# The delta-rule mixer in four streams, laid under the convolutions, with the inverse's second orientation transposed from the first

## The reference

```python
def gated_deltanet_mixer(h, w_in, conv_w, a_log, dt_bias, norm_w, w_out):
    B, T, _ = h.shape
    H, Dh = GDN_HEADS, GDN_HEAD_DIM                      # 8 heads of 128
    proj = h @ w_in                                      # qkv 3072, z 1024, b 8, a 8
    ...
    qkv = jax.nn.silu(causal_dwconv(qkv, conv_w))        # width 4
    ...
    q = l2norm(q) * (Dh ** -0.5)
    k = l2norm(k)
    beta = jax.nn.sigmoid(b.astype(jnp.float32))
    g = -jnp.exp(a_log.astype(jnp.float32)) * jax.nn.softplus(
        a.astype(jnp.float32) + dt_bias.astype(jnp.float32))
    o = chunk_gated_delta_rule(q, k, v, g, beta)
    o = rmsnorm_2(o, norm_w) * jax.nn.silu(z.reshape(B, T, H, Dh))
    return o.reshape(B, T, GDN_V_DIM) @ w_out
```

## Time and profile before

| | us |
|---|---|
| median of 3 runs | 3209.63 (3208.53 to 3215.67) |
| the profiled execution | 3211.74 |
| its span | 3210.0 |
| PE busy | 2693.5 (84%) |
| DVE busy | 883.0 (28%) |
| ACT busy | 405.9 (13%) |

### The profile page before, as it was taken

One profiled execution on the slowest core, in us unless ns is written; L12 is line 12 of the kernel. 1 busy time (PEld: TensorE's weight loads), 2 busy tenths in 40 slices (PEclk: granted clock), 3 DMA queues, 4 the chain that ended last, 5 costly groups with the idle time before them and its releaser, 6 DMA issues.

```text
span 3210.0 us, 34641 instructions
## 1 busy us (share of the span) xinstructions
PE 2693.5 (84%) x13970; PEld 1520.1 (47%) x13970; DVE 883.0 (28%) x1880; ACT 405.9 (13%) x767; POOL 203.5 (6%) x267
## 2 busy tenths in 40 slices
PE   6987877789989987899799888888794779887886
PEld 3443445444444444544385434434664755444443
DVE  3144627510120045200224110110545544111111
ACT  1121212110010013100101000000122111000001
POOL 3111101110010020100011000000000001000000
PEclk9998997899999999999899998999897989989999
DMA  6655649254444441334543799999530025899997
GB/s 225 211 197 195 228 173 323 70 178 143 139 146 154 157 147 53 138 120 154 215 162 140 307 419 421 419 420 418 165 106 1 5 96 199 365 416 421 421 421 309
DMA packets 264854, 721.85 MB, mean 225 GB/s; under 512 B 15248, under 2 KB 149040, under 8 KB 210864
## 3 DMA queue, kind: packets, MB, share of 16 engines
q1 hardware_dynamic: 251232, 690.00, 56.4%
q0 software_dynamic: 13520, 30.41, 2.8%
HBM read 719.17 MB, written 1.18 MB: 224 GB/s over the span
## 4 chain that ended last, share of the span: by engine, by line
PE 65%; DMA 20%; DVE 9%; SPq 2%; issue 2%; ACT 2%; DVEq 0%; ACTq 0%
PE ps L872 22%; DMA ring<-in_moe_w_up 16%; PE ps L1496 9%; PE ps L982 7%; PE ps L897 5%; PE ps L1083 3%; PE ps L1065 3%; DMA ring<-in_ada_w 3%; SPq L532 2%; PE ps L1037 2%; DMA ring<-in_ffn_w_in 1%; PE ps L908 1%; PE ps L877 1%; PE ps L1486 1%; PE ps L1268 1%
## 5 line engine op out<-in xcount | busy, mean ns | idle before, releaser
L872 PE MATMUL ps<-ring,hT 128*128 128x512 f32 x1600 | 717.6, 603 | 49.7 <-DMA ring<-in_ffn_w_in 30.2
L872 PEld LDWEIGHTS ps<-ring,hT 128*128 128x128 f32 x1600 | 305.6, 194 | 417.2 <-issue 404.6
L1496 PE MATMUL ps<-arena 128*32 128x512 f32 x1536 | 275.8, 699 | 82.0 <-DMA ring<-in_moe_w_up 76.0
L1496 PE MATMUL ps<-ring,arena 128*32 128x512 f32 x512 | 275.1, 700 | 0.0
L1486 PEld LDWEIGHTS ps<-arena,h 128*128 128x128 f32 x1024 | 248.4, 334 | 15.3 <-issue 11.7
L1486 PE MATMUL ps<-arena,h 128*128 128x128 f32 x1024 | 244.9, 398 | 3.5 <-issue 3.5
L982 PE MATMUL ps<-ring,arena 128*128 128x512 f32 x528 | 232.2, 593 | 2.4 <-ACT arena L1725 2.4
L2162 DVE SCALAR_TENSOR_TENSOR arena<-ps,arena 128x256 f32<-128x256 f32 x66 | 28.1, 425 | 614.1 <-ACT arena L1721 613.9
L1496 PEld LDWEIGHTS ps<-arena 128*32 128x32 f32 x1536 | 67.6, 125 | 263.8 <-issue 180.7
L897 PE MATMUL ps<-hT,ring 128*128 128x256 f32 x768 | 171.3, 387 | 1.5 <-ACT hT L1659 1.5
L1037 PE MATMUL ps<-ring,cond 128*2 128x128 f32 (+1 forms) x3072 | 110.6, 307 | 66.7 <-DMA ring<-in_ada_w 61.7
(11 more groups left out here) (484 smaller groups left out, 2648.1 us busy)
## 6 DMA issues: line engine op xcount, KB each, us to landing
ring<-in_moe_w_down SPq DMA_DIRECT2D x128, 1024.0 KB, 17.7
ring<-in_ada_w SPq DMA_DIRECT2D x48, 2048.0 KB, 13.2
arena<-in_moe_w_gate SPq DMA_DIRECT2D x96, 1024.0 KB, 11.7
arena<-in_moe_w_up SPq DMA_DIRECT2D x96, 1024.0 KB, 9.8
ring<-in_ffn_w_in SPq DMA_DIRECT2D x66, 1024.0 KB, 8.6
ring<-in_ffn_w_out SPq DMA_DIRECT2D x33, 1024.0 KB, 5.0
ring<-in_moe_w_gate SPq DMA_DIRECT2D x32, 1024.0 KB, 15.7
ring<-in_moe_w_up SPq DMA_DIRECT2D x32, 1024.0 KB, 17.8
```

The source lines that it names most:

```text
L872: m = pe.matmul(o3, lhsT_of(k), ring[:, a:a + 2, k * EH:(k + 1) * EH], start=start and k == 0, stop=stop and k == KC - 1)
L1496: m = pe.matmul(ps[a * CAP:(a + 1) * CAP, 6, :].rearrange("p (u c) -> p u c", u=2), x_slots[:, k, a * CAP:(a + 1) * CAP], slot_pair(gate_s ...
```

## The change

The same mixer is written in another order and in parts with other operations.

- Under the 24 projection blocks now also run: b and a, the decays, their sums and running sums, the turning of finished q, k, v groups to tokens (`tokens_turned`), the squares for the norms (now on ACT, L2120 of the new program) with their sums, and the differences of the decays (`gap`). DVE makes block c's convolution before it gates block c - 1, the sigmoid has two buffers, and the note copies are gone.
- The four z blocks stand between the turnings and the scores instead of in one piece.
- All four pairs of head group and tile are streams (s = 0 to 3) of one run of levels. The first level has no products: D and DT are the identity less LM and less its transpose, which PE turns (`unit_turned`).
- From level 2 on only `D - D T` is a matmul. Its transpose, which the step needs as weights, is made by PE transposing D itself (`inverse_turned`) and an ACT copy. At the last level only the transposed result is made.
- The copies after the levels go to ACT. For tile 1 `q S` is scaled afterwards, not q before.
- The multiplication of z by the norm weights moves under the levels. Tile 0 of the output is projected before tile 1 is turned, and `arena_passed_on` is signalled after tile 1 is turned.
- The scratch of the streams also takes v_scale, v_shift and two tiles of x_sb.

```diff
-            for c in range(12):
...
+            def tokens_turned(g):
+                pe.wait_ge(sem("gd_conv"), 4 * g + 4)
+                for t in range(2):
+                    transposes([gT[:, 4 * g + q, t * P:(t + 1) * P] for q in range(4)])
+
+            def features_turned(t):
+                pe.wait_ge(sem("gd_norm"), t + 1)
+                for where, off in ((gtok, 8), (gkb, 0), (gtok, 0)):
+                    for hd in (0, 4):
+                        transposes([where[:, t, off + hd + a, :] for a in range(4)])
+
+            for j in range(12):
                 feature_major(SEQ, NT)
-            token_major(LAT)
-            token_major(LAT)
-            pe.wait_ge(sem("gdn_constants"), 16 * 6)
+                if j >= 2 and j % 2 == 0:
+                    tokens_turned(j // 2 - 1)
...
+            def unit_turned(s):
+                pe.wait_ge(sem("gd_lm"), LM_TURNED[s])
+                for a in range(4):
+                    m = pe.transpose(ps[:, 2 * s, a * P:(a + 1) * P], LM[s][:, a, :], ident[:, :])
+                m.then_inc(sem("gd_t"), 1)
+
+            def t_of(lvl, s):
+                pe.wait_ge(sem("gd_lm"), d_ready(lvl, s))
+                each(2 * s, lambda a: LM[s][:, a, :], lambda a: DD[s][:, a, :]).then_inc(sem("gd_t"), 1)
+
+            def inverse_turned(s):
+                for a in range(4):
+                    m = pe.transpose(ps[:, 2 * s + 1, a * P:(a + 1) * P], DD[s][:, a, :], ident[:, :])
+                m.then_inc(sem("gd_t"), 1)
+
+            def step_of(lvl, s):
+                pe.wait_ge(sem("gd_t_read"), turned_read(lvl, s))
+                if lvl + 1 < LEVELS:
+                    m = each(2 * s, lambda a: DT_[s][:, a, :], lambda a: TT[s][:, a, :])
+                else:
+                    m = each(2 * s + 1, lambda a: TT[s][:, a, :], lambda a: DT_[s][:, a, :])
+                m.then_inc(sem("gd_step"), 1)
+
+            z_block(0, 0)
+            tokens_turned(5)
+            z_block(0, 1)
+            features_turned(0)
+            z_block(1, 0)
+            pe.wait_ge(tp_evacuated, n.tp)
+            pe.wait_ge(sem("gd_gap"), 4)
+            scores(0)
+            scores(1)
+            features_turned(1)
+            unit_turned(0)
+            unit_turned(1)
+            z_block(1, 1)
+            pe.wait_ge(tp_evacuated, n.tp)
+            pe.wait_ge(gu_evacuated, n.gu)
+            scores(2)
+            scores(3)
+            t_of(1, 0)
+            t_of(1, 1)
+            unit_turned(2)
+            step_of(1, 0)
+            step_of(1, 1)
+            unit_turned(3)
+            t_of(1, 2)
+            t_of(1, 3)
+            step_of(1, 2)
+            step_of(1, 3)
+            for lvl in range(2, LEVELS):
+                for s in range(4):
+                    t_of(lvl, s)
+                for s in range(4):
+                    inverse_turned(s)
+                for s in range(4):
+                    step_of(lvl, s)
+
...
+                if t == 1:
+                    mixed_tiles(g_o, (1,))
+                    pe.wait_ge(tp_evacuated, n.tp)
+                    pe.matmul(ps[:, 4, 0:1], ident[:, :], ident[:, 0:1], start=True, stop=True).then_inc(sem("arena_passed_on"), 1)
+                for half in range(2):
+                    m = mixer_half(out_slots, t, half, t * P)
...
-                for lvl in range(LEVELS):
-                    for t in range(2):
-                        s0 = 2 * (LEVELS * g + lvl) + t
-                        pe.wait_ge(sem("gd_lm"), s0 + 1)
-                        for a in range(4):
-                            m = pe.matmul(ps[:, 3 * t, a * P:(a + 1) * P], LM[t][:, a, :], DD[t][:, a, :], start=True, stop=True)
-                        m.then_inc(sem("gd_t"), 1)
-                    for t in range(2):
-                        s0 = 2 * (LEVELS * g + lvl) + t
-                        pe.wait_ge(sem("gd_t_read"), s0 + 1)
-                        for a in range(4):
-                            pe.matmul(ps[:, 3 * t + 1, a * P:(a + 1) * P], DT_[t][:, a, :], TT[t][:, a, :], start=True, stop=True)
-                        for a in range(4):
-                            m = pe.matmul(ps[:, 3 * t + 2, a * P:(a + 1) * P], TT[t][:, a, :], DT_[t][:, a, :], start=True, stop=True)
-                        m.then_inc(sem("gd_step"), 1)
...
+            for lvl in range(1, LEVELS):
+                for s in range(4):
+                    act.wait_ge(sem("gd_t"), t_done(lvl, s))
+                    tell(nc.scalar.copy(TT[s], quarter(ps[:, 2 * s, :])), sem("gd_t_read"))
+                for s in range(4 if lvl >= 2 else 0):
+                    act.wait_ge(sem("gd_t"), t_done(lvl, s) + 4)
+                    tell(nc.scalar.copy(DT_[s], quarter(ps[:, 2 * s + 1, :])), sem("gd_t_read"))
...
-                tell(V.tensor_copy(note[:, :], eps_t[0:1, :]), sem("gd_pre"))
...
+            for c in range(24):
+                conv(c)
+                if c >= 1:
+                    conv_gated(c - 1)
+                if c == 4:
+                    ba_read()
+                if c == 6:
+                    decays_made()
+                if c == 11:
+                    sums_read()
+                if c in (13, 14):
+                    squares_summed(c - 13)
+                if 17 <= c < 21:
+                    gap(c - 17)
+                if c in (21, 22):
+                    squares_summed(c - 19)
+            conv_gated(23)
...
+            def scores_read(s):
+                dve.wait_ge(sem("gd_scores"), s + 1)
+                do(V.tensor_tensor(LT[s], b4(2 * s), LM[s], ALU.mult))
+                do(V.tensor_tensor(AT[s], b4(2 * s + 1), AT[s], ALU.mult))
+                tell(V.tensor_tensor(LM[s], LT[s], all4(lv[:, 0, :]), ALU.mult), sem("gd_lm"))
+
+            def first_level(s, turned):
+                tell(V.tensor_tensor(DT_[s], all4(ident[:, :]), LM[s], ALU.subtract), sem("gd_lm"))
+                dve.wait_ge(sem("gd_t"), turned)
+                tell(V.tensor_tensor(DD[s], all4(ident[:, :]), b4(2 * s), ALU.subtract), sem("gd_lm"))
+                tell(V.tensor_tensor(LM[s], LT[s], all4(lv[:, 1, :]), ALU.mult), sem("gd_lm"))
...
+            for lvl in range(1, LEVELS):
+                for pair in ((0, 1), (2, 3)):
+                    for s in pair:
+                        if lvl + 1 < LEVELS:
+                            dve.wait_ge(sem("gd_t"), t_done(lvl, s))
+                            tell(V.tensor_tensor(LM[s], LT[s], all4(lv[:, lvl + 1, :]), ALU.mult), sem("gd_lm"))
+                    for s in pair:
+                        dve.wait_ge(sem("gd_step"), step_done(lvl, s))
+                        if lvl + 1 < LEVELS:
+                            tell(V.tensor_tensor(DD[s], DD[s], b4(2 * s), ALU.subtract), sem("gd_lm"))
+                        else:
+                            tell(V.tensor_tensor(DT_[s], DT_[s], b4(2 * s + 1), ALU.subtract), sem("gd_inverse"))
+                if lvl in (2, 3):
+                    zt = g_z[:, lvl - 2, :].rearrange("p (a b) -> p a b", a=8)
+                    do(V.tensor_tensor(zt, zt, g_norm.rearrange("p (o b) -> p o b", o=1).broadcast_to([P, 8, P]), ALU.mult))
+
             for g in range(2):
```

More of the change, by code:

```diff
@@ new lines, in _, with z_block, each @@
+            z_units = [n.slots(2), n.slots(2)]
+            def z_block(half, t):
+                if t == 0:
+                    for s in z_units[half]:
+                        filled(s)
+                products(gu_bank(), lambda k: hT[:, k, SEQ + t * P:SEQ + (t + 1) * P], z_units[half]).then_inc(block_done, 1)
+            def each(bank, lhsT, rhs):
+                for a in range(4):
+                    m = pe.matmul(ps[:, bank, a * P:(a + 1) * P], lhsT(a), rhs(a), start=True, stop=True)
+                return m
@@ L1642, in _ @@
+            n.x += 2
             moe(1)
@@ new lines, in taken @@
+            def taken(dst, bank, count, done):
+                act.wait_ge(*count)
+                tell(nc.scalar.copy(dst, quarter(ps[:, bank, :])), done)
+            taken(TT[0], 0, (sem("gd_u"), 1), sem("gd_u_read"))
+            taken(TT[1], 2, (sem("gd_u"), 2), sem("gd_u_read"))
+            for g in range(2):
+                taken(TT[2 + g], 4 + 2 * g, (sem("gd_u"), 2 * g + 3), sem("gd_u_read"))
+                taken(LM[g], 1 + 2 * g, (sem("gd_u"), 2 * g + 4), sem("gd_u_read"))
+            for g in range(2):
+                taken(LM[2 + g], 5 + 2 * g, (sem("gd_o"), 2 * g + 1), sem("gd_batch"))
+                taken(g_o0[:, 4 * g:4 * g + 4, :], 2 * g, (sem("gd_o"), 2 * g + 2), sem("gd_batch"))
@@ L2873, in _ @@
[L2873 to L2876 removed]
+            z_gated(1, 1)
+            first_level(0, 1)
+            first_level(1, 2)
+            scores_read(2)
+            scores_read(3)
+            first_level(2, 5)
+            first_level(3, 6)
```

413 lines of the change are left out of this document (203 added, 210 removed).

## The result

| us | before | after |
|---|---|---|
| median | 3210.38 (4 runs, 3208.53 to 3215.67) | 3085.82 (4 runs, 3077.52 to 3091.33) |
| profiled execution | 3211.74 | 3081.46 |
| its span | 3210.0 | 3079.7 |

The ratio is 0.9607 with an interval of 0.9579 to 0.9635: 125 us less. I had forecast 3087.

A forecast was written before the change was run, and what follows sets the result against it. It took TensorE to bound the conv stretch and levels, VectorE parts between. Mixer 98.5 + 58.2 + 44.9 + 21.2 + 34.9 = 257.7 against 382.3, 124.3 less after rounding: 3087 us, range 3079 to 3094.

The forecast's parts named there:

- Step 1: Convolution stretch: 86.1 us of projections plus 12.4 of inserted TensorE work, 98.5 us; at most 3 more for table loads.
- Step 2: From the last conv projection to the first four-stream level: 58.2 us, TensorE's z blocks covering other work, then VectorE bounding.
- T: The end of the last conv projection block, 2363.97 us before the change and forecast at 2376.
- Step 3: Five levels of four streams, bound by TensorE: 9.3 us for the first, 8.9 for four more, 44.9 instead of 95.
- Step 4: Levels' end to first gated tile: ten TensorE groups and three dependent hops to 12.8 us, then VectorE, 21.2 us.
- Step 5: Output, from the gated tile to the mixer's end: two projections, slow start and tile 1's turning, 34.9 us.
- Behind: Stretch from the mixer's end to the end: stays 549.8 us despite the later signal for expert loads.
- (a): Rival: TensorE's clock falls in the joints, six pauses at 2 us each, 3099 us; chance 0.17.
- (b): Rival: levels stay bound by hand-offs, 68 us in place of 44.9, total 3110 us; chance 0.05.
- (c): Rival: the experts' loads are late, up to 15 us given back, 3102 us; chance 0.05.
- (d): Rival: a turned group in the levels costs as much as a matmul group, 3096 us; chance 0.07.
- (e): Rival: slower than before, clock stays at 1.2 GHz from the conv stretch on, near 3300 us; chance 0.03.

The follow-up runs named there:

- e_z_first: Changed kernel with all four z blocks in one piece ahead of the turning of normed q and k; median 3088.98 us, mixer 262.23 us.
- e_matmul_inverse: Changed kernel with the inverse's second orientation at levels 1 to 5 made by matmul group and VectorE subtraction; median 3096.06 us, mixer 265.18 us.
- e_warm_matmul: Changed kernel with seven unread matmul groups filling TensorE's pause ahead of the first output tile's turning; median 3087.65 us, output 32.20 us.
- e_pairs: Changed kernel with levels 2 to 6 run for streams 0 and 1 first, then 2 and 3; median 3094.64 us, mixer 267.35 us.
- e_not_under: Changed kernel with b/a, decays, first five turned pairs, squares and gaps behind the 24 projection blocks; median 3096.22 us, mixer 268.00 us.

## Why the prediction was right, point by point

- **Step 1, conv stretch 98.5.** 98.78. TensorE stands once, 1.06 us, for a convolution held up by ScalarE's table loads (forecast: 0 to 3, and 0 in the sum); in return the work added to the stretch was 11.8 us in the chain and not 12.4 (b and a 3.48, five pairs 4.35, small sums 0.35, running sums 3.57). Two small errors cancel.
- **Step 2, 58.2.** 58.1, by its own working partly for a wrong reason: z blocks as cover (e_z_first). TensorE's first longer wait comes at T+42.3, as worked out. TensorE's rows of the waits in steps 1 and 2:

```profile
2311.35 3.72 PE L908 MATMUL ps<-hT,ring 128*128 128x256 f32 x16 [1.06 <-DVE arena L2883]
...
2413.24 3.81 PE L1611 MATMUL ps<-arena 128*128 128x128 f32 x32 [1.65 <-DVE arena L2960]
...
2424.01 1.16 PE L1611 MATMUL ps<-v_scale,arena 128*128 128x128 f32 x8 [1.46 <-DVE arena L2985]
2426.19 1.16 PE L1611 MATMUL ps<-x_sb 128*128 128x128 f32 x8 [1.01 <-DVE x_sb L2985]
```

- **Step 3, 44.9.** 45.2, a level 8.90. TensorE bounds it: taking 0.45 us per group away from it or giving it back moves a level by just that (e_matmul_inverse). The turned group, for which there was no row, costs 0.44; I had taken 0.43.
- **Step 4, 21.2.** 21.0, by another path than the one told. I had ten groups of TensorE and three hops up to 12.8 us, where VectorE's part begins. TensorE goes through 16 groups there without a pause; the chain leaves it after 13 of them, 11.6 us, and one subtraction brings it to 12.5. The groups that I left out stood in for two of the hops: that is luck.
- **Step 5, 34.9.** 34.93, with the slow start of 16.6 in the sum (16.0 measured) and shown to be the clock (e_warm_matmul); the turning of tile 1 took 2.2 and not 1.8. Here too small errors cancel.
- **Behind, 549.8.** 549.6. That this agrees to 0.2 is luck, since it scatters by some 3 us; that it did not grow is the result. The argument for it was half right: the 13.9 us that are left of the signal's lead suffice, and the experts do have room. The one that needed it was the shared expert, which I had called safe; with no lead it costs 14.6 us. VectorE's wait for v_scale of 4.36 us is gone, as forecast, but it lay under the output projection, and nothing shows that it was worth anything.
- **Rivals.** (a) the clock falling in the joints: it stayed at 1.00 from T to 2478, through all the pauses there. The slow group that I named for it, in the earlier trace rows, is not the one right behind the pause, which took 1.16, but one that starts 2.4 us after it. But the clock did fall, in two of 12 profiles, where I had not looked: at the b and a products that the change puts between projection blocks, for 3.4 us. The mechanism was real, the place and the size were not. (b) is answered by e_pairs: two streams would be bound by hops, four are not. (c) and (d) did not come, (e) neither.
- **What of the 124 us is tested.** Undone one at a time: setup under the convolutions 10.0, four streams 9.4, turned orientation 7.2, split output 4.3, place of z 0.3; in all 31. The remaining 93 are accounted for by the rows alone. The largest is the 57.6 us in which TensorE worked 20.9, at a clock of 0.63, where the new stretch from T to the levels has 1.00; two levels without or nearly without cost, the lighter hops from 6.79 to 5.41, and one passage through scores, solution and state where there were two are others. The setup and the z blocks can cover for each other, so their single effects don't add up to what both are worth; undoing both was not tried.

## What to carry to other kernels

A chain of small dependent products is sped up by more independent streams only up to the point where the engine's own work fills the loop; work out both numbers before adding streams (two streams were held at 5.4 us by hand-offs with 4.4 of work; four have 8.9 of work and wait for none), and from there on only fewer or cheaper instructions help. Here a signal that lets loads start early was worth what stood behind those loads in the same queue, not what they themselves feed: look at the order of issue and at the share just ahead of each first use, not at the mean DMA share. Judge edits of a few microseconds by a stretch of the profile that repeats within 0.1 us, when whole executions differ by 14.

## What the runs showed of the hardware

- TensorE's clock can fall while the engine is never idle: with 32 products of 16 columns (3.47 us at a clock of 1.00) it read 0.79 under them and 0.59 in the next block, in two of 12 profiles and not in the other ten. In both, the slow start ahead of them was the longest of the 12. What decides between them stays open.
- A pause of 6.56 us brought it to 0.50 behind it, and 2.7 us were lost; one of 6.02 in e_not_under was followed by 5.6 us at 0.60. Pauses of 1.0 to 1.7 us between T and the levels left it at 1.00, while before a pause of 1.83 us was followed, 2.4 us after its end, by a slow group.
- 56 transposes right behind matmuls, with nothing else on TensorE, kept it at 1.00 for 6.3 us.
- Six loads of 1 MB and a share of DMA time of 0.64 in the 69 us behind them look like room; the same six, 14 us later and still ahead of the shared expert's loads, cost 14.6 us. The share was 0.99 in just the 26.35 us that mattered.
